# Giving the turns of y score banks, and moving VectorE's y and low-weight work one step later

## The reference, cut to what matters

```python
for l in range(DEPTH):
    h = rms_norm(x, norm_g[l]) * (1 + sc[:, None]) + sh[:, None]
    qa, ka, va, ga, qb, kb, vb, gb, qn, kn, vn, gn = split_proj(h @ w_in[l])
    ...
    y = jnp.concatenate([ya, yb, yn], axis=-1) @ w_out[l]
    ...
    x = x + gt[:, None] * y
# second block
y = gmlp_mixer(h, ...)               # layer 0
y = dilated_attention_mixer(h, ...)  # layer 1: o * silu(z), then y @ w_out
x = x + rms_norm_2(y, norm_post[i])
```

## Time and profile before

| | |
|---|---|
| three executions | 1204.38, 1209.5 and 1209.1 us; median 1209.1 us |
| the profiled execution | 1208.92 us |
| its span, first to last instruction | 1207.1 us |
| TensorE busy with matmuls | 1120.6 us, 93% of the span |
| VectorE, ScalarE busy | 726.2 us, 600.8 us |
| mean granted TensorE clock | 0.977 of full |
| DMA | 157.94 MB, 131 GB/s over the span |

### The profile page before, as it was taken

The page is one execution under the profiler, slowest core; times in us unless marked ns, Lnnn a source line. Parts: engine busy times, 40 slices in busy tenths (PEclk is TensorE's granted clock), DMA queues, the critical chain, the costliest instruction groups (busy, mean ns, idle before and its releaser), DMA issues.

```text
span 1207.1 us, 16741 instructions
## 1 busy us (share of the span) xinstructions
PE 1120.6 (93%) x5877; PEld 894.5 (74%) x5877; DVE 726.2 (60%) x1320; ACT 600.8 (50%) x1176; POOL 261.5 (22%) x324
## 2 busy tenths in 40 slices
PE   5989999999989989999897999999799999999997
PEld 1666677767668777787676887888688888888785
DVE  3488876777763764753447586664656646555543
ACT  3345454444762546644654544453554454445552
POOL 2582421181006150321202031000122202111101
PEclk8999989998999999999999999999899999999999
DMA  8756453425013233232205756555366664443301
GB/s 331 165 175 204 127 151 107 131 87 149 28 53 101 78 105 88 71 88 70 70 2 185 255 157 190 159 174 192 111 204 176 190 192 125 121 140 122 106 1 53
DMA packets 79291, 157.94 MB, mean 131 GB/s; under 512 B 5793, under 2 KB 6089, under 8 KB 78953
## 3 DMA queue, kind: packets, MB, share of 16 engines
q1 hardware_dynamic: 75880, 147.41, 39.2%
q0 software_dynamic: 3328, 9.46, 3.4%
HBM read 153.73 MB, written 3.11 MB: 130 GB/s over the span
## 4 chain that ended last, share of the span: by engine, by line
PE 75%; DVE 9%; ACT 5%; issue 4%; POOL 3%; DMA 2%; SPq 0%; DVEq 0%; ACTq 0%; POOLq 0%
PE bank L771 18%; PE bank L773 17%; PE bank L772 17%; PE bank L920 5%; PE bank L895 3%; PE bank L905 3%; PE bank L996 3%; DVE w_lo L1732 2%; PE bank L969 2%; DVE work L1752 2%; POOL small L1534 2%; PE bank L981 2%; PE bank L791 1%; ACT w_hi L1123 1%; DMA work<-in_w_ada_dram 1%
## 5 line engine op out<-in xcount | busy, mean ns | idle before, releaser
L771 PE MATMUL bank<-w_lo,h_hi 128*128 128x512 f32 (+1 forms) x1152 | 458.6, 398 | 25.9 <-DVE h_lo L1801 10.1
L773 PE MATMUL bank<-w_hi,h_hi 128*128 128x512 f32 (+1 forms) x1152 | 444.1, 386 | 0.0
L772 PE MATMUL bank<-w_hi,h_lo 128*128 128x512 f32 (+1 forms) x1152 | 443.9, 385 | 0.0
L1732 DVE TENSOR_TENSOR w_lo<-raw,w_hi 128x1024 fp32r<-128x1024 f32 x224 | 286.7, 1286 | 171.7 <-ACT w_hi L1123 170.7
L1123 ACT ACTIVATE w_hi<-raw 128x1024 fp32r<-128x1024 f32 x224 | 235.8, 1057 | 270.4 <-PE bank L773 233.7
L771 PEld LDWEIGHTS bank<-w_lo,h_hi 128*128 128x128 f32 x1152 | 220.2, 191 | 75.7 <-issue 27.1
L773 PEld LDWEIGHTS bank<-w_hi,h_hi 128*128 128x128 f32 x1152 | 219.6, 191 | 44.2
L772 PEld LDWEIGHTS bank<-w_hi,h_lo 128*128 128x128 f32 x1152 | 220.4, 191 | 38.8
L920 PE MATMUL bank<-work,stage 128*128 128x128 f32 x640 | 90.7, 282 | 0.0
L1720 POOL TENSOR_TENSOR stage<-stage 128x512 f32<-128x512 f32 x24 | 42.3, 1785 | 217.6 <-DVE stage L551 217.6
L920 PEld LDWEIGHTS bank<-work,stage 128*128 128x128 f32 x640 | 81.7, 197 | 1.0 <-issue 0.2
(11 more groups left out here) (177 smaller groups left out, 1115.6 us busy)
## 6 DMA issues: line engine op xcount, KB each, us to landing
raw<-in_b_w_in_dram SPq DMA_DIRECT2D x80, 512.0 KB, 3.7
raw<-in_w_in_dram SPq DMA_DIRECT2D x56, 512.0 KB, 4.2
raw<-in_a_w_in_dram SPq DMA_DIRECT2D x48, 512.0 KB, 4.0
raw<-in_w_ada_dram SPq DMA_DIRECT2D x32, 512.0 KB, 3.7
work<-in_w_ada_dram SPq DMA_DIRECT2D x16, 512.0 KB, 11.4
raw<-in_w_out_dram SPq DMA_DIRECT2D x16, 512.0 KB, 3.5
raw<-in_a_w_out_dram SPq DMA_DIRECT2D x16, 512.0 KB, 3.5
raw<-in_b_w_out_dram SPq DMA_DIRECT2D x8, 512.0 KB, 3.5
```

The source lines that it names most:

```text
L771: pe.matmul(bank, hT(h_hi, ph, at, tt), w_lo[:, s, k, lo:lo + w], start=first, stop=False)
L772: pe.matmul(bank, hT(h_lo, ph, at, tt), w_hi[:, s, k, lo:lo + w], start=False, stop=False)
L773: mm = pe.matmul(bank, hT(h_hi, ph, at, tt), w_hi[:, s, k, lo:lo + w], start=False, stop=last)
L1732: dve.tensor_tensor(w_lo[:, i % SPLIT, :, :], raw[:, PIECE_AT[p] % RAW, :, :], w_hi[:, i % SPLIT, :, :].bitcast(F32), ALU.subtract).then_i ...
```

## The change

Four things change.

1. In the attentions, a turn of y takes the bank of the score ring that the next score would take, not bank 6 (first half) or 7 (second half). The step is an odd one in all cases, right behind the scores of a pair: the first halves in layer 0 in steps 45, 47, 51 and 53 rather than 44, 45, 46 and 47, and in layer 1 in 23 and 25 rather than 23 and 24. The second halves stay in steps 49, 55 and 61 (layer 0) and 29 (layer 1).
2. The splits of the first output pieces in layer 0 go from steps 45, 47, 49 and 51 to 46, 48, 50 and 52.
3. VectorE does the `y` and `split` tasks of step i in step i+1, behind that step's maximum and weighing and ahead of its output. ScalarE does them in step i, as before.
4. In the dilated attention both tiles of the first half are turned in step 19 (before: 19 and 20), into the next two ring banks, with VectorE's parts in step 20; and the second halves of both tiles, which shared bank 7, now take 6 and 7.

```diff
-HALF_TURNED = {19: 0, 20: 1}
+HALF_TURNED = {19: X_TILES}
...
-    for i, tt in enumerate(tts):
-        tasks.setdefault(first + i, []).append(("y", tt, 0))
+    for i, tt in zip((45, 47, 51, 53) if layer == 0 else (23, 25), tts):
+        tasks.setdefault(i, []).append(("y", tt, 0))
...
-        tasks.setdefault(first + 1 + (2 if layer == 0 else 1) * i, []).append(("split", i))
+        tasks.setdefault(first + (2 + 2 * i if layer == 0 else 1 + i), []).append(("split", i))
...
-            def y_turn(ph, src, tt, q):
-                bank = take(pe, 6 + (tt if ph == "gout" else q) % 2, "y", ph, tt, q)
+            def y_turn(ph, src, tt, q, at=None):
+                if at is None:
+                    at = 6 + (q if ph in ("out0", "out1") else tt)
+                bank = take(pe, at, "y", ph, tt, q)
...
-                            y_turn(f"out{layer}", gate, *task[1:])
+                            ring = SCORE_BANKS + (2, 3)
+                            y_turn(f"out{layer}", gate, *task[1:], at=ring[s_use[0] % len(ring)])
...
-                        y_turn("dout", dgate, HALF_TURNED[i], 0)
+                        ring = SCORE_BANKS + (2, 3)
+                        for k, tt in enumerate(HALF_TURNED[i]):
+                            y_turn("dout", dgate, tt, 0, at=ring[(s_use[0] + k) % len(ring)])
...
                     if 0 <= i < len(units):
                         weigh(units[i])
+                    for task in fill.get(i - 1, ()):
+                        if task[0] == "y":
+                            y_part(f"out{layer}", *task[1:])
+                        if task[0] == "split":
+                            split_until(SPLIT_AT[(f"out{layer}", 0, 0)] + task[1] + 1)
...
                     for task in tasks:
                         if task[0] == "products":
                             ada_products(task[1])
-                        if task[0] == "y":
-                            y_part(f"out{layer}", *task[1:])
-                        if task[0] == "split":
-                            split_until(SPLIT_AT[(f"out{layer}", 0, 0)] + task[1] + 1)
```

8 lines of the change are left out of this document (4 added, 4 removed).

## The result

| | before | after |
|---|---|---|
| median | 1207.16 us of 4 | 1195.39 us of 4 |
| lowest to highest | 1204.38 to 1209.5 us | 1193.34 to 1198.85 us |
| span of the profiled execution | 1207.1 us | 1192.6 us |
| mean granted TensorE clock | 0.977 | 0.98 |

The ratio of the times is 0.9903, with a 95% interval from 0.9876 to 0.9929: 11.7 us faster, between 8.6 and 15.0. The fourth execution of before lowered its median by 2 us against the one that the forecast stood on. Of all executions behind this document one, of the kernel with the banks alone, took 1857.14 us at a mean granted clock of 0.556, and is left out of its ratio.

The account below looks back on a forecast made before the run. TensorE, busy in 93% of the span, was taken as the bound, so only its waits could give time. Gains of 3.9 + 1.4 + 2.3 + 1.5 = 9.1 us took 1209.1 to 1200.0 us, range 1195 to 1206.

Parts of the forecast that it names:

- Layer 0: Step 43's scores to the first output product: 43.3 to 39.4 us, 3.9 us gained, bounds 0 and 8.9.
- TensorE resumes 0.15 us after the release: Layer 0 pairs: once VectorE's y part frees the bank, TensorE starts 0.15 us later, making a pair with a turn 4.81.
- VectorE's chain: Layer 0, steps 47 and 49: maximum, w_lo, output, second maximum, y part to 5.46, TensorE at 5.61; such a pair costs 5.6.
- Splits: Layer 0: moving them a step or two costs nothing beyond the 1.15 us already in the chain.
- Layer 1: Two pairs gain 0.8 us and step 29's second half 0.6: 1.4 together, bounds 0.5 and 2.3.
- dilated attention: Scores of step 19 to those of step 21: 7.66 us becomes 5.4, bounds 5.3 and 6.5; 2.3 us gained.
- last product: Last output product: the second turn starts 0.5 us after the first, not 2.02, in its own bank; 1.5 us gained.
- The sum: Whole kernel: 3.9 + 1.4 + 2.3 + 1.5 = 9.1 us gained, from 1209.1 to 1200.0 us.
- The rule on emptying the pipeline: VectorE's links in the pairs: taken strictly, each is 0.08 us longer, gain 1.6 us less, time 1201.6.
- Half the gain: Rival, 2 in 10: layer 0's score guard costs about what the old waits cost; gain 4.2 us, time 1204.9.
- All waits vanishing: Rival, 1 in 8: second maximum starts earlier, so the guard costs nothing; gain 15.1 us, time 1194.
- The slower one: Rival, 1 in 20: score waits for y part, next maximum for score, over twelve turns; 15.4 us lost, time 1215.

Follow-up runs that it names:

- the early splits: Changed kernel with the four weight splits of layer 0's steps 44 to 50 moved to steps 32 to 38; 1199.27 us, ratio 0.9943 to before.
- the other bank: Changed kernel with turns of y in the ring bank of the next pair's second score, not the first; 1194.84 us, ratio 0.9899 to before.

## Why the prediction was right, point by point

**What bounds the kernel.** The waits named in the earlier trace rows were the ones that went. The times of eleven kernels follow from the lengths of these stretches within about 2 us, so on the whole little was given back or added outside of them. A single trace is no proof of that: from layer 0's product to layer 1's step 23 the traces have 241.5 to 244.3 us, and from layer 1's product to step 19 of the dilated attention 512.5 to 516.4. From before to after these went from 241.56 to 242.74 and from 516.25 to 515.00, which cancels.

**Layer 0: the mechanism was right, the size 0.8 us too small.** The waits stand where they were forecast, in front of scores and of the first product, and lie between 0.33 and 1.09 us. The pairs took 3.86, 4.71, 5.47, 5.46, 4.04, 3.81, 3.37, 2.18, 2.19 and 3.52 us, where I had 3.9, 4.8, 5.6, 5.6, 4.2, 3.9, 3.5, 2.2, 2.2 and 3.5. The step that was mis-sized is the 0.15 us in "TensorE resumes 0.15 us after the release": I had read it in front of turned probabilities. In front of a score it is 0.06 (320.87 + 0.67 = 321.54, and the score starts at 321.60). That difference of 0.09 in six pairs is 0.5 of the 0.8; the rest is VectorE's y part, 0.67 for 0.69, w_lo with its successor after 1.12 for 1.15, and in the short pairs the way through both engines, 1.95 for 1.99 (338.37 to 339.63 + 0.69).

**VectorE's chain.** It came out to a few hundredths: from the start of pair 47, w_lo after 2.30 us (forecast 2.29), the output after 3.42 (3.44), the second maximum after 3.61 (3.64), the y part after 4.74 (4.77). ScalarE was in time for the y part and for the w_lo shown, as assumed. The run with the y part moved back shows how near that was: 1.1 us earlier, h_hi is not there, and VectorE waits 0.88 and 0.49 us for it.

**Splits.** That w_lo costs some 0.8 us in a pair is shown by the early splits, where pairs 47 and 49 fell from 5.47 to 4.70. That their move delayed nothing else fits: the first product waits for h_lo and not for weights, and from there to layer 1's step 23 TensorE stands still for 13.0 us, against 13.2 before.

**Layer 1, dilated attention, last product.** 1.7 for 1.4, where the two pairs of 4.70 for 4.81 are the resume time again; 2.3 for 2.3; 1.6 for 1.5. The last two were also measured alone: 3.3 us with an interval of 1.3 to 5.2.

**The sum.** 10.3 us by the trace for 9.1; the three comparisons gave 11.7, 11.1 and 9.4, with a mean of 10.7. The predicted 1200.0 us stands 4.6 over the first median and 2.0 over the third. Some 2 us of that is the start: the kernel before has medians of 1206.75, 1206.42 and 1207.37 us in sets of 24, 17 and 17, not the 1209.1 of three executions. 1.2 us is the sum's own shortfall. What is left is within the spread of executions. The range held narrowly: its lower end is 1195, and the first median lies 0.4 us above it.

**The rule on emptying the pipeline.** By it the gain would have been 1.6 us less, 1201.6. In the trace after, the output starts 1.12 us after a w_lo of 1.21, and the next instruction 0.59 after a y part of 0.67. The Trainium skill, VectorE: DVE Perf Modes, section "The DRAIN you can't avoid", read as whole lengths laid end to end, does not agree with that; the shorter gap held.

**The rivals.** Half the gain fell: layer 0 gave 4.7 us. All waits vanishing fell as well, though the other bank, at 36.28 us, brought layer 0's stretch 2.3 us of the remaining 4.2 nearer to its 34.4. The slower one had its place right: a score that waits for a y part, in the bank that a turn has taken. The banks alone are that case, 6.2 us slower, since there turns stand in even steps, right ahead of the scores. "Both scores of a pair are issued before the turn" is what kept it away, and that is the work of the new steps.

**What the forecast missed.** It priced four sets of waits, and never asked what each part of the change does by itself. In layer 0 banks alone cost 4.0 us, steps alone 6.1 and both together 2.6; VectorE's order alone gains 1.9, and with the steps it loses 2.0. Each of these holds one fall of the clock, the third two, so at full clock VectorE's order alone would gain up to 3.5, an estimate from these lengths; but it gives 0.85 back in layer 1. The three together gain 4.7 in layer 0 and 1.7 in layer 1, more than any part does. The sum could come out because it was made for the finished order, and not part by part.

## What to carry to other kernels

Where a side task borrows a bank, ask which instruction wants the bank next, and follow the chain that frees it through every engine, in each engine's own order; here the banks alone and the steps alone cost 6.2 and 9.8 us, VectorE's order alone was within noise of nothing, and the three together gained. Price the finished order from pair to pair, by starts of rows, and then try the other free bank: a guard on the second of two scores that run side by side cost 2.3 us less of a stretch here than one on the first, though the whole time didn't show it clear of the noise. A half of a split placed earlier is not free because its own engine has room: what counts is what stands behind the other half on ScalarE.

## What the runs showed of the hardware

**The same program reaches the same point at different times.** Up to step 43 nothing differs between before and after, yet its scores start at 317.18 in the one and at 313.03, 313.78 and 317.58 us in the other. Part of it is TensorE's clock. The busy time of each engine in two stretches, in the kernel before (PE, PEld, DVE, ACT, POOL; then the granted clock, the DMA share and GB/s):

```profile
240.00:260.00 20.00, 20.00 (x107) 15.74 (x107) 15.64 (x29) 6.51 (x18) 14.84 (x17) 1.00 0.26 81
260.00:280.00 20.00, 17.12 (x85) 14.05 (x85) 11.10 (x21) 9.71 (x23) 16.14 (x39) 0.83 0.25 79
```

The second stretch in the changed kernel:

```profile
260.00:280.00 20.00, 17.12 (x102) 13.62 (x102) 13.66 (x27) 11.60 (x25) 13.96 (x35) 0.91 0.31 87
```

TensorE was busy without a gap at full clock (2.4 GHz) from 240 to 260 us, and then stood still for some 3 us in 20, as much in both executions; the clock fell to the lower level (1.2 GHz) for part of that time, for longer in the one than in the other: 0.83 against 0.91, and 0.74 in the first repetition of the changed kernel. The sixteen small matmuls of the row sums took, in the timeline of TensorE of the kernel before:

```profile
272.11 3.54 PE L698 MATMUL bank<-ones,work 128*128 128x1 f32 x16 [0.94 <-DVE work L1752]
```

and of the changed kernel:

```profile
269.70 1.92 PE L698 MATMUL bank<-ones,work 128*128 128x1 f32 x16 [0.94 <-DVE work L1757]
```

Why it falls for longer in some executions stays open. It explains 1.6 of the 4.15 us by which these two starts differ (3.54 - 1.92); 2.4 were there when the row sums began, and the stretches ahead of them were not followed up. Nor does the clock of this stretch decide the start: in that repetition, with 0.74, the row sums began at 267.73 and step 43's scores at 313.78.

**One fall of the clock, 1.6 us.** The stretch of layer 0 took 43.27 and 44.89 us in two kernels that are the same there, at a granted clock of 1.00 throughout and of 0.50 from 335 to 338 us. TensorE had just stood still for 2.59 us in both.

**TensorE resumes at several speeds** behind the same VectorE instruction: 0.06 us after the end of h_lo in front of a score, 0.15 us in front of turned probabilities (321.92 + 0.67 = 322.59 against 322.74, in the run without the banks), and 0.21 us in front of the first product (350.74 + 0.69 = 351.43 against 351.64). A turn of y, a transposition like the turn of probabilities, resumes after 0.06 us as well (in the last product of the kernel before), so it isn't the transposition that makes the difference. What does was not tried.

**A wait can hide inside a group.** With the other bank no idle time is shown in front of any score of these pairs, and the group's length, 1.52 or 1.90 us for 1.13, holds it.
